# Delta rule on the chunks' own 64 columns, in quarters of the array, and split operands at multiples of 128 floats

## The reference, cut to what matters

```python
a_low = jnp.where(strict, jnp.einsum('bhnid,bhnjd->bhnij', kb, k) * decay, 0.0)
ia = a_low + jnp.eye(c, dtype=q.dtype)
u = lax.linalg.triangular_solve(ia, v * beta[..., None], left_side=True, lower=True, unit_diagonal=True)
w = lax.linalg.triangular_solve(ia, kb * jnp.exp(gc)[..., None], left_side=True, lower=True, unit_diagonal=True)
qk = jnp.einsum('bhnid,bhnjd->bhnij', q, k) * decay
...
    v_new = u_n - jnp.einsum('bhcd,bhde->bhce', w_n, state)
    o_n = jnp.einsum('bhcd,bhde->bhce', qg_n, state) + jnp.einsum('bhij,bhje->bhie', qk_n, v_new)
    state = state * gl_n[..., None, None] + jnp.einsum('bhcd,bhce->bhde', kd_n, v_new)
```

## Time and profile before

| what | value |
| --- | --- |
| median of 3 runs | 939.32 us (939.04 to 940.88) |
| the profiled execution | 939.73 us, span in the trace 937.8 us |
| TensorE busy | 896.4 us (96%), 5474 records |
| VectorE, ScalarE, GpSimd busy | 557.0, 430.7, 61.6 us |
| TensorE's mean granted clock | 0.989 of 2.4 GHz |

### The profile page before, as it was taken

How to read it: one execution, slowest core, us unless ns; L and a number is a source line. 1 busy time by engine, 2 the same in 40 slices (tenths; PEclk the granted TensorE clock), 3 DMA queues, 4 the chain that set the end, 5 groups by cost and what they waited for, 6 DMA issues and landing times.

```text
span 937.8 us, 13178 instructions
## 1 busy us (share of the span) xinstructions
PE 896.4 (96%) x5474; PEld 783.2 (84%) x5474; DVE 557.0 (59%) x794; ACT 430.7 (46%) x577; POOL 61.6 (7%) x72
## 2 busy tenths in 40 slices
PE   5999999999999999999699999999989899999996
PEld 5998999899998888887599998787877788888885
DVE  4855564564657566555469789654366556666442
ACT  6644444743345444444365524753433444444341
POOL 1000000000030000000100163100000000000000
PEclk9999999999999999999999999999999999999999
DMA  9557744455455445556467645004564466655441
GB/s 301 176 197 209 229 141 136 145 166 177 135 180 180 156 160 180 166 197 215 138 207 148 163 102 179 1 1 136 140 218 138 155 194 189 191 184 184 157 157 45
DMA packets 127489, 151.75 MB, mean 162 GB/s; under 512 B 16919, under 2 KB 93078, under 8 KB 127430
## 3 DMA queue, kind: packets, MB, share of 16 engines
q1 hardware_dynamic: 127290, 150.83, 51.7%
q0 software_dynamic: 64, 0.07, 0.0%
q10 hardware_dynamic: 76, 0.02, 0.0%
HBM read 148.80 MB, written 3.68 MB: 163 GB/s over the span
## 4 chain that ended last, share of the span: by engine, by line
PE 87%; DVE 8%; ACT 2%; issue 1%; POOL 0%; DMA 0%; ACTq 0%; POOLq 0%; DVEq 0%
PE bank L486 25%; PE bank L487 24%; PE bank L488 24%; DVE w_lo L1779 2%; DVE arena L2118 1%; PE bank L551 1%; PE bank L920 1%; PE bank L938 1%; ACT w_hi L1301 1%; PE bank L632 1%; PE bank L612 1%; PE bank L731 1%; PE bank L969 1%; PE bank L950 1%; PE bank L1140 1%
## 5 line engine op out<-in xcount | busy, mean ns | idle before, releaser
L1779 DVE TENSOR_TENSOR w_lo<-ring,w_hi 128x2048 fp32r<-128x2048 f32 (+2 forms) x133 | 301.3, 2270 | 197.4 <-ACT w_hi L1301 197.2
L1301 ACT ACTIVATE w_hi<-ring 128x2048 fp32r<-128x2048 f32 (+2 forms) x133 | 250.0, 1881 | 142.4 <-PE bank L488 128.7
L486 PE MATMUL bank<-h_hi,w_hi 128*128 128x256 f32 (+1 forms) x640 | 184.8, 289 | 4.3 <-DVE w_lo L1779 3.0
L488 PE MATMUL bank<-h_hi,w_lo 128*128 128x256 f32 (+1 forms) x640 | 181.7, 284 | 0.0
L487 PE MATMUL bank<-h_lo,w_hi 128*128 128x256 f32 (+1 forms) x640 | 181.7, 284 | 0.0
L486 PE MATMUL bank<-w_hi,h_hi 128*128 128x512 f32 (+1 forms) x400 | 155.7, 389 | 0.7 <-DVE h_lo L1816 0.7
L488 PE MATMUL bank<-w_hi,h_lo 128*128 128x512 f32 (+1 forms) x400 | 152.7, 382 | 0.0
L487 PE MATMUL bank<-w_lo,h_hi 128*128 128x512 f32 (+1 forms) x400 | 152.4, 381 | 0.0
L486 PEld LDWEIGHTS bank<-h_hi,w_hi 128*128 128x128 f32 (+1 forms) x640 | 122.9, 192 | 7.3 <-DVE w_lo L1779 3.4
L487 PEld LDWEIGHTS bank<-h_lo,w_hi 128*128 128x128 f32 (+1 forms) x640 | 123.0, 192 | 0.7 <-issue 0.5
L488 PEld LDWEIGHTS bank<-h_hi,w_lo 128*128 128x128 f32 (+1 forms) x640 | 122.9, 192 | 0.0
(11 more groups left out here) (315 smaller groups left out, 1242.2 us busy)
## 6 DMA issues: line engine op xcount, KB each, us to landing
ring<-in_w_in SPq DMA_DIRECT2D x60, 1024.0 KB, 5.2
ring<-in_w_gate_up SPq DMA_DIRECT2D x44, 512.0 KB, 4.6
ring<-in_w_down SPq DMA_DIRECT2D x10, 1024.0 KB, 5.1
ring<-in_w_mem_kv SPq DMA_DIRECT2D x8, 1024.0 KB, 6.6
ring<-in_w_gla_out SPq DMA_DIRECT2D x4, 1024.0 KB, 5.0
ring<-in_w_x_out SPq DMA_DIRECT2D x4, 1024.0 KB, 5.0
ring<-in_w_dsa_out SPq DMA_DIRECT2D x4, 1024.0 KB, 5.3
ring<-in_w_o SPq DMA_DIRECT2D x4, 1024.0 KB, 5.1
```

The lines of the kernel that those rows point to most:

```text
L486: mm(o, ah, bh, start=start, stop=False, skip_group_check=True)
L488: return mm(o, al, bh, start=False, stop=stop, skip_group_check=True)
L1301: act(w_hi[:, k % NHI, 0:m], ring[:, order.index(name) % NSLOT, 0:m], ACT.Copy)\
L1779: tt_(w_lo[:, i, 0:m], ring[:, i, 0:m], w_hi[:, k % NHI, 0:m].bitcast(F), ALU.subtract)\
```

## The change

It has two parts. First, the matrices kg, qg, nA, nAm, qkT, Tm, TmT and zst keep only the chunk's own 64 columns: rows 0 to 63 hold the first chunk of the tile, rows 64 to 127 the second. Each product becomes two of 64 by 64 per head: rows 0 to 63 of the array into partitions 0 to 63 of a bank, rows 64 to 127 into partitions 64 to 127 of the same bank, one chunk after the other in the program. kg and qg contract over 128 rows and split only the columns. The transposes t0 and tm become products with the identity's block. u and gd move 128 columns per quarter; wt contracts over one chunk's 64 rows, writes 128 partitions, and has one bank per chunk c in place of one per tile t, both filled in one pass after u; its copies on ScalarE follow both copies of u. Constants (level masks, chunk mask, identity) are 64 columns wide; ScalarE, VectorE and GpSimd work on half as many elements, except that `decays` makes eight subtractions on [64, 2, 64]. Second, the regions of the arena are put in another order and rounded so that every split tile begins at a multiple of 128 floats.

```diff
+        def aligned():
+            end[0] = -(-end[0] // 128) * 128
...
-        nA, qkT = tiled(nA_at, 8, 128), tiled(qkT_at, 8, 128)
+        nA, qkT = tiled(nA_at, 8, CH), tiled(qkT_at, 8, CH)
...
-                    for h in range(4):
-                        ins = mm(bank[:, 128 * h:128 * h + 128], cv[:, 4 + h, 128 * t:128 * t + 128],
-                                 cv[:, a + h, 128 * t:128 * t + 128], start=True, stop=True)
+                    for h, c in itertools.product(range(4), range(2)):
+                        q = slice(128 * t + 64 * c, 128 * t + 64 * c + 64)
+                        ins = mm(bank[64 * c:64 * c + 64, 64 * h:64 * h + 64], cv[:, 4 + h, q], cv[:, a + h, q],
+                                 start=True, stop=True)
...
+            def chunk_products(bank, stationary, moving, t):
+                for h, c in itertools.product(range(4), range(2)):
+                    r = slice(64 * c, 64 * c + 64)
+                    ins = mm(bank[r, 64 * h:64 * h + 64], stationary[r, 4 * t + h, :], moving[r, 4 * t + h, :],
+                             start=True, stop=True)
+                return ins
+            def chunk_transposes(bank, src, t):
+                for h, c in itertools.product(range(4), range(2)):
+                    r = slice(64 * c, 64 * c + 64)
+                    ins = mm(bank[r, 64 * h:64 * h + 64], src[r, 4 * t + h, :], ident[r, r], start=True, stop=True)
+                return ins
...
-                    for h in range(4):
-                        ins = mm(bank[:, 128 * h:128 * h + 128], nAm[n % 2][:, 4 * t + h, :], TmT[:, 4 * t + h, :],
-                                 start=True, stop=True)
-                    done(f"lz{n}{t}", ins)
+                    done(f"lz{n}{t}", chunk_products(bank, nAm[n % 2], TmT, t))
...
-                bank = open_bank(f"wt{t}")
-                for h in range(4):
-                    ins = mm(bank[:, 128 * h:128 * h + 128], kbe[:, 4 * t + h, :], TmT[:, 4 * t + h, :], start=True, stop=True)
-                done(f"wt{t}", ins)
+            for c in range(2):
+                open_bank(f"wt{c}")
+            for i, c in itertools.product(range(8), range(2)):
+                r = slice(64 * c, 64 * c + 64)
+                ins = mm(bank_of(f"wt{c}")[:, 64 * i:64 * i + 64], kbe[r, i, :], TmT[r, i, :], start=True, stop=True)
+                if i == 7:
+                    done(f"wt{c}", ins)
...
-                m = const("lev")[:, 128 * n:128 * n + 128].unsqueeze(1).broadcast_to([128, 8, 128])
+                m = const("lev")[:, CH * n:CH * n + CH].unsqueeze(1).broadcast_to([128, 8, CH])
                 nc.gpsimd.tensor_tensor(nAm[n % 2], nA, m, ALU.mult).then_inc(signal("level_mask"), 1)
...
-                    tt_(TmT[:, s, :], TmT[:, s, :], by_head(f"xt{n}{t}"), ALU.add).then_inc(reader(f"xt{n}{t}"), 1)
+                    tt_(TmT[:, s, :], TmT[:, s, :], by_chunk(f"xt{n}{t}"), ALU.add).then_inc(reader(f"xt{n}{t}"), 1)
```

More of the change, by code:

```diff
@@ L81, in shape_constants, with own_chunk @@
     put("after", same & (p > f))
+    def own_chunk(full):
+        return np.where(p < CH, full[:, :CH], full[:, CH:])
+    put("id64", own_chunk(p == f))
+    put("chunk64", own_chunk(p <= f))
     lev = []
@@ L891, in _ @@
                 bank = open_bank(f"t0{t}")
-                for h in range(4):
-                    ins = nc.tensor.transpose(bank[:, 128 * h:128 * h + 128], nAm[0][:, 4 * t + h, :], ident)
-                done(f"t0{t}", ins)
+                done(f"t0{t}", chunk_transposes(bank, nAm[0], t))
             w = (plain_unit("w1k"), plain_unit("w1v"))
@@ L926, in level @@
                     bank = open_bank(f"tm{n}{t}")
-                    for h in range(4):
-                        ins = nc.tensor.transpose(bank[:, 128 * h:128 * h + 128], TmT[:, 4 * t + h, :], ident)
-                    done(f"tm{n}{t}", ins)
+                    done(f"tm{n}{t}", chunk_transposes(bank, TmT, t))
             def level_end(n):
@@ L936, in level_end @@
                     bank = open_bank(f"xt{n}{t}")
[L937 to L940, removed]
+                    done(f"xt{n}{t}", chunk_products(bank, Tm, zst, t))
             def nsa_logits(p):
@@ L1088, in gdn_out @@
                     bank = open_bank(f"gd{t}")
-                    for h in range(4):
-                        mm(bank[:, 128 * h:128 * h + 128], qkT[:, 4 * t + h, :], v_new[:, 4 * t + h, :],
+                    for h, c in itertools.product(range(4), range(2)):
+                        r = slice(64 * c, 64 * c + 64)
+                        mm(bank[r, 128 * h:128 * h + 128], qkT[r, 4 * t + h, :], v_new[r, 4 * t + h, :],
                            start=h == 0, stop=False, skip_group_check=True)
@@ L1634, in _ @@
                 copy(f"u{t}", u_tok[:, 4 * t:4 * t + 4, :].rearrange("p a b -> p (a b)"))
-                copy(f"wt{t}", wT[:, 4 * t:4 * t + 4, :].rearrange("p a b -> p (a b)"))
+            for c in range(2):
+                copy(f"wt{c}", wT[:, 8 * c:8 * c + 8, :].rearrange("p a b -> p (a b)"))
             nsa_step(15)
@@ L2091, in decays @@
                 for j in range(2):
-                    for t in range(TT):
-                        src = halves(f"gb{j}")[:, :, 128 * t:128 * t + 128]
-                        gc = cols[:, t, 12 + 2 * j:14 + 2 * j].unsqueeze(2).broadcast_to([128, 2, 128])
-                        ins = tt_(nA[:, 4 * t + 2 * j:4 * t + 2 * j + 2, :], src, gc, ALU.subtract)
+                    for t, c in itertools.product(range(TT), range(2)):
+                        r, at = slice(64 * c, 64 * c + 64), 128 * t + 64 * c
+                        gc = cols[r, t, 12 + 2 * j:14 + 2 * j].unsqueeze(2).broadcast_to([64, 2, CH])
+                        ins = tt_(nA[r, 4 * t + 2 * j:4 * t + 2 * j + 2, :], halves(f"gb{j}")[r, :, at:at + 64], gc,
+                                  ALU.subtract)
                     ins.then_inc(reader(f"gb{j}"), 1)
@@ L2209, in _ @@
                 ve.wait_ge(*full(f"t0{t}"))
-                tt_(TmT[:, 4 * t:4 * t + 4, :], by_head(f"t0{t}"), ident.unsqueeze(1).broadcast_to([128, 4, 128]), ALU.add)\
+                tt_(TmT[:, 4 * t:4 * t + 4, :], by_chunk(f"t0{t}"), ib[:, 0:4, :], ALU.add)\
                     .then_inc(reader(f"t0{t}"), 1)
```

66 lines of the change are left out of this document (39 added, 27 removed).

## The result

| | before | after |
|---|---|---|
| median, us | 939.18 (937.66 to 940.88, 4 runs) | 929.28 (927.24 to 929.62, 4 runs) |
| profiled execution, us | 939.73 | 927.24 |
| its span, us | 937.8 | 925.4 |

The ratio is 0.989, with a 95% interval of 0.987 to 0.991: 9.9 us less where 11.5 were forecast (927.8). On a second chip the same kernel took 928.11 us (6 runs) against 938.64: 0.989 again.

What follows compares the result with a forecast made beforehand. The prediction took TensorE's stream of records as the bound. From the profiled 939.73 us it took 5.0 for addresses and 6.65 for quarters, giving 928.1, less 0.41 to the median: 927.8 us, range 924.5 to 934.5.

Steps and rivals of the forecast that it cites:

- Addresses: Products on split tiles moved to multiples of 128 floats: faster records save 5.0 us, between zero and 5.9.
- Before kwvc: TensorE's wait for w_lo ahead of weight unit kwvc: w_lo comes 0.6 us earlier, gain 0.6 us.
- kg and qg: Two quartered products between full-array work: 0.89 - 0.33 us saved each, gain 1.1 us.
- t0: Transposes turned into 32 quarter records: a loss of 0.15 us.
- lz1: First lz product as quarters, up to the first scores: gain 0.8 us.
- The stretch where VectorE is late: From the first scores to 590.6 us: halved level additions and mask on VectorE and GpSimd gain 2.0 us.
- Level 4: Steady delta-rule level of 11.4 us: shorter lz, xt and additions gain 1.4 us.
- Level 3: Delta-rule level whose last mask was expected to hold VectorE's normalisation: only 0.5 us of gain remains.
- Level 5, u and wt: Two gains of 0.89 us, less some 0.9 for array visits and 0.3 for ScalarE's copy order: gain 0.5 us.
- gd: The gd product issued as quarter pairs: a loss of 0.1 us.
- a gain absorbed by VectorE and ScalarE: Rival: the normalisation chain keeps its pace and only part of the quarters' gain reaches the end, 931 us; chance 0.08.
- the quarters in turn: Rival: row halves writing one PSUM bank take turns instead of running side by side, 941.6 us; chance 0.10.

Runs made afterwards that it cites:

- mask experiment: The changed kernel with each of GpSimd's level masks made a second time after the first; 928.73 us, beside 928.11 for the changed kernel on that chip.
- fewer visits: The changed kernel with qg's products right behind kg's, and np15's transposes and copy ahead of wt's; 927.15 us, ratio 0.988.
- the quarters alone: The changed kernel with the arena regions laid out as before the change; 931.88 us, ratio 0.993.
- partners apart: The changed kernel with the loops of lz and xt exchanged, all four heads of one quarter before the other quarter; 931.52 us in one run.

## Why the prediction held, and where it was off

- Addresses, 5.0. M, Y and F give 0.3, 1.3 and 1.7; mg, z, oT and m2 (which the prediction counts under m) the rest: the excess per record over 226.7 ns, before less after, times the records is 5.3, less 0.3 for m's 256 columns: 5.0. By the medians 4.3. The pace of 226.7 held for all but y and z, which stay 1.2 and 1.0 ns above it. That h's row would be the new state was right; that a multiple of 128 floats is what it takes was not tested by the step, and is too strict: 64 do.
- Before kwvc, 0.6: measured 0.54. From the copy ahead of the subtractions to w_lo's start VectorE took 3.92 us before (lines 2088 to 1779) and 3.39 after (2120 to 1811). The eight subtractions took 2.42 us against 1.41 for four, 1.0 more and not 0.3 to 0.5, but, as the step had it, beside GpSimd's product; the two halved operations behind them took 0.48 and 0.43 against 1.74 and 0.69.
- kg and qg, 1.1: 1.02, two of 0.51. t0, -0.15: -0.19. lz1, 0.8: 0.70.
- The stretch where VectorE is late, 2.0: 1.72 from the first logits to step 3's. TensorE waits there 1.05 and 1.71 us ahead of lines 750 and 1052 after the change.
- Level 4, 1.4: 1.50. That is what the step's chain over xt and the additions gave.
- Level 3, 0.5: 1.51 (11.41 to 9.90). This term was mis-sized, by 1.0 us, because its mechanism was wrong. The collision came as foreseen (line 2040 at 588.93 beside the mask), but the step took it to delay the last normalisation, for which TensorE waits. It delays the one before, done at 590.61, whose probabilities line 750 reads only at 592.24, TensorE's timeline of level 3:

```profile
589.50 0.87 PE L750 MATMUL bank<-arena 128*128 128x128 f32 x6
590.31 0.93 PE L975 MATMUL bank<-arena 64*128 64x128 f32 x8
591.16 1.15 PE L880 MATMUL bank<-arena 64*64 64x64 f32 x32
592.24 0.55 PE L750 MATMUL bank<-arena 128*128 128x128 f32 x3
```

  The mask experiment bounds the slack: the first 0.9 us are free, the next 1.1 cost 0.34. The error was not in the stall but in who reads its result.
- Level 5, u and wt, 0.5: 0.51, with 0.49 instead of 0.3 lost to np15's copy behind wt's; the order with fewer visits got exactly this back. gd, -0.1: -0.13.
- Sum of the quarters: 6.65 forecast, 7.2 by the stretches. Of the rivals, a gain absorbed by VectorE and ScalarE is out, as levels 3 and 4 shortened by 1.5 us each, and so are the quarters in turn. The rule of the Trainium skill, TensorEngine Tiling (Array Packing), Gotcha 1: PSUM Pressure, is not what happens here: the pairs are of different row halves and write one bank, and 16 of them pass in 0.93 us. The 62 ns per MATMUL of the same skill's TensorE: Matmul & The Clock Gate, Wait — 56ns, not 53.3ns?, are for a sequencer that decodes each MATMUL itself. They don't bound these records, which start 0.93/31 = 30 ns apart; no run shows how this chip decodes them.
- Terms that add to 12.2 and a median that moved 9.9: what was missed is not in the changed work. The part from the first product on oT to the first on f, windows (us, TensorE busy and records, granted clock, DMA share, GB/s) of before, after and the quarters alone:

```profile
682.99:867.70 184.71, 177.77 (x801) 0.98 0.56 180
...
673.64:857.04 183.40, 176.31 (x802) 0.98 0.55 181
...
677.40:865.20 187.80, 180.53 (x801) 0.96 0.55 177
```

By the records that took twice their usual pitch, time lost at 1.2 GHz in that part is about 1.5 us in before, 1.1 in after and 4.5 in the quarters alone; in the traces of the other variants it is 1.1, 1.3 or 2.6 to 3.4, with the same work. The range had 1.6 us for this, and the predicted time none. The executions without a trace have a granted clock on record too, and it answers the question. Of after's four, the traced one took 927.24 us at a clock of 0.988; the others took 929.62, 929.60 and 928.95 at 0.985, 0.985 and 0.987. At an equal clock the two kernels lie about 12 us apart. In the rounds of the later experiments six runs of before at 0.985 took 941.3 to 942.9, and eight at 0.988 took 939.4 to 940.1. Eleven at 0.990 took 938.1 to 939.2, against 925.65 for after on the second chip. So the change is worth about 12 us of work, as its terms say, and the first median of after stands high because three of its four runs had a lower clock, by some 2 us (an estimate, from 927.24 to the others). That the median came within 1.5 us of the forecast is luck in part: level 3 gave 1.0 us more than forecast and the clock took about 2 back. What gives one execution more time at 1.2 GHz than another, no run shows.

A second such part follows TensorE's wait of 7.32 us for VectorE at the start of the second block: its first product on h (line 505) comes at 470.59 us in after and at 470.44 in the kernel with fewer visits, the window from 470 to 480 has a granted clock of 1.00 in the one and 0.74 in the other, and kwvc starts at 517.52 and 519.36, 1.84 us later with the same work between.

## What to carry to other kernels

Compare stretches between landmarks that the change can't move, not whole times: here four of five repeat to 0.02 or 0.1 us, where medians blur by 1 to 2, and a part's gain is read off the one stretch that has it. See first how far a stretch wavers by itself: one of the five did so by some tenths. And compare whole times at an equal granted clock. When an operation is held by another engine, follow its result to its reader before you price the stall. And when a gain leaves a wait as long as it was, look for independent work that stands behind that wait in the same queue: moving one call ahead of another gave 2.6 us, a quarter of what the whole change gave.

## What the runs showed of the hardware that I had not expected

- Products of 512 fp32r columns take 226.8 to 227.9 ns a record if stationary and moving tile both start at a multiple of 64 floats (256 bytes), and 229.7 to 233.3 ns at the other offsets tried (16, 32, 40, 56, 96); one tile of a triple off a multiple is enough. Products of 256 columns take 120.0 ns at multiples and 117.8 ns with the high weights off one. I had taken the first to be the stationary side's alone, and the second for noise.
- Two diagonal 64 by 64 quarters writing one bank run side by side, 58 ns the pair. A quarter may start about four records ahead of its turn in the queue: with partners apart a step of 32 records took 1.32 us from first to last start, not 0.93 nor 1.86.
- From the last record on the full array to the first on the quarters (kg) pass 0.21 us, where 0.12 passed before the change, and 0.15 from the last quarter's record to the next on the full array; one visit saved gave 0.34 us.
- A VectorE product of two columns takes 0.16 us alone and 1.09 beside a GpSimd product of 1.27 us. Not every operation is held: the reciprocal at 588.74 us, beside the same product, took 0.16.
